# Two attentions and two gate pairs: copies moved behind exponentials, one sum moved ahead of others

## What is computed

```
h = layer_norm(x)
proj = h @ w_in                       # pool, conv, q, kv, k_rope and the logits of three gates
gates = sigmoid(g_logits + b_gate)    # three gates, 1024 wide each: 24 tiles of 128, 12 pairs
y_pool = pool_mixer(u_pool) @ pool_proj        # sliding means minus input, mixed by group
y_conv = conv_module(u_conv) @ conv_proj       # 31 taps, layer norm, silu
y_mla = attention(8 heads, chunk-causal, 64 wide values) @ mla_proj
merged = gates[0] * y_pool + gates[1] * y_conv + gates[2] * y_mla
h = layer_norm(a * h + merged @ w_out)
...                                   # mixture of experts, then a state-space mixer and a conv FFN
h = fox_attention(h)                  # 16 heads, causal, with forget gates
...                                   # output projection, norm, conv FFN, norm
```

## Time and profile before

| | |
|---|---|
| median of 3 runs | 2550.92 us (2550.4 to 2553.96) |
| profiled execution | 2549.24 us |
| its span | 2547.4 us |
| TensorE products busy | 2515.7 us, 99% |
| VectorE busy | 1374.1 us, 54% |
| ScalarE busy | 618.7 us, 24% |
| GpSimd busy | 83.7 us, 3% |
| granted TensorE clock | 0.998 of full |
| first attention | about 173 to 226 us of the span |
| gate pairs | about 219 to 455 us |
| second attention | about 1953 to 2064 us |

### The profile page before, as it was taken

How to read it: one execution, slowest core, us unless ns; L and a number is a source line. 1 busy time by engine, 2 the same in 40 slices (tenths; PEclk the granted TensorE clock), 3 DMA queues, 4 the chain that set the end, 5 groups by cost and what they waited for, 6 DMA issues and landing times.

```text
span 2547.4 us, 31452 instructions
## 1 busy us (share of the span) xinstructions
PE 2515.7 (99%) x10720; PEld 1903.6 (75%) x10720; DVE 1374.1 (54%) x2528; ACT 618.7 (24%) x1406; POOL 83.7 (3%) x117
## 2 busy tenths in 40 slices
PE   9999999999999999999999999999999999999998
PEld 7857878684444467888746888888885668888887
DVE  6778754441111146646385777752361857777633
ACT  3244223120000013222222222210231633222112
POOL 0010000000000010000020000000000200000000
PEclk9999999999999999999999999999999999999999
DMA  4224212248999952222112222224322022222233
GB/s 143 83 81 184 91 61 97 91 182 305 363 336 336 327 187 71 84 90 91 59 50 99 83 83 90 82 91 132 108 89 78 9 67 91 90 83 91 84 117 130
DMA packets 90562, 319.06 MB, mean 125 GB/s; under 512 B 9632, under 2 KB 13856, under 8 KB 90432
## 3 DMA queue, kind: packets, MB, share of 16 engines
q1 hardware_dynamic: 81584, 284.37, 32.4%
q10 hardware_dynamic: 5152, 19.92, 2.0%
q0 software_dynamic: 3728, 13.44, 1.6%
HBM read 295.61 MB, written 22.02 MB: 125 GB/s over the span
## 4 chain that ended last, share of the span: by engine, by line
PE 91%; DVE 5%; ACT 2%; issue 1%; DMA 1%; POOL 0%; ACTq 0%; SPq 0%; DVEq 0%; POOLq 0%
PE bank L924 44%; PE bank L650 13%; PE bank L1198 13%; PE bank L896 4%; PE bank L1069 2%; PE bank L776 2%; PE bank L798 1%; PE bank L1477 1%; PE bank L1347 1%; PE bank L1465 1%; PE bank L825 1%; ACT R L1601 1%; DVE R L3106 1%; PE bank L684 1%; PE bank L1210 1%
## 5 line engine op out<-in xcount | busy, mean ns | idle before, releaser
L924 PE MATMUL bank<-SQ,arena 128*128 128x256 f32 x2040 | 469.8, 379 | 0.0
L924 PEld LDWEIGHTS bank<-SQ,arena 128*128 128x128 f32 x2040 | 387.5, 190 | 52.8 <-DVE arena L2167 0.2
L1198 PE MATMUL bank<-arena 128*128 128x512 f32 x768 | 332.7, 592 | 0.8 <-ACT arena L1844 0.8
L924 PE MATMUL bank<-X,ring 128*128 128x256 f32 x1360 | 322.5, 379 | 0.0
L650 PE MATMUL bank<-arena,ring 128*128 128x256 f32 (+1 forms) x1280 | 319.5, 411 | 0.0
L650 PEld LDWEIGHTS bank<-arena,ring 128*128 128x128 f32 x1280 | 243.2, 190 | 74.9 <-issue 46.6
L924 PEld LDWEIGHTS bank<-X,ring 128*128 128x128 f32 x1360 | 258.2, 190 | 38.4 <-issue 3.6
L1198 PEld LDWEIGHTS bank<-arena 128*128 128x128 f32 x768 | 144.6, 190 | 176.5 <-issue 176.5
L924 PE MATMUL bank<-X,arena 128*128 128x256 f32 x680 | 160.9, 379 | 2.0 <-DVE bank L2189 2.0
L924 PE MATMUL bank<-SQ,ring 128*128 128x256 f32 x680 | 161.1, 380 | 1.2 <-DVE R L2194 0.9
L2189 DVE TENSOR_TENSOR bank<-bank,arena 128x256 f32<-128x256 f32 x97 | 41.9, 432 | 223.1 <-ACT bank L1681 222.8
(11 more groups left out here) (394 smaller groups left out, 3038.8 us busy)
## 6 DMA issues: line engine op xcount, KB each, us to landing
ring<-w_stream SPq DMA_DIRECT2D x326, 512.0 KB, 3.3
arena<-w_stream SPq DMA_DIRECT2D x204, 512.0 KB, 5.1
y_slots<-X ACTq DMA_DIRECT2D x1, 9216.0 KB, 25.8
y_slots<-arena ACTq DMA_DIRECT2D x16, 512.0 KB, 5.1
x_tok<-arena ACTq DMA_DIRECT2D x1, 2048.0 KB, 6.6
out_t<-X SPq DMA_DIRECT2D x16, 128.0 KB, 2.2
X<-x_t SPq DMA_DIRECT2D x1, 1024.0 KB, 8.2
part<-params SPq DMA_DIRECT2D x1, 824.0 KB, 8.9
```

The source lines that it names most:

```text
L924: mm = pe.matmul(out, w(n), v(k), start=start and n == 0, stop=n == len(chunk_pairs(p)) - 1, skip_group_check=not start)
L1198: mm = pe.matmul(ebank(t)[:, :], w_, ERING[:, at:at + S], start=(k == 0), stop=(k == len(lhs) - 1))
```

## The change

Four places are touched.

1. "att": on ScalarE `early()` keeps the latent's value copies, and the pooled chunks with the fill's transfer become `pooled_chunks`, called as `later()` behind both parts of the second head's exponentials.
2. "fatt": on TensorE the last of the six value steps moves from the first extra part to the second one, between the scores of heads 1 and 2. On ScalarE the value copies move from `early()` to `later()`.
3. Both: GpSimd copies the queries of head 2 ahead of its wait for the values.
4. Gate pairs 0 and 8: VectorE makes the third sum ahead of the branch inputs' and next weights' sums. In pair 0 the next pair's weight sums and the branch's sums of weights go behind the fourth output; in pair 8 the weight sums stay ahead of it and the branch's go behind it. The order in the other pairs stays.

```diff
-            attention("fatt", lambda: more_values(2, C8), None,
+            attention("fatt", lambda: more_values(2, C8 - 1), lambda: more_values(C8 - 1, C8),
...
-            def attention(name, early):
+            def attention(name, early, later=None):
...
-                early()
+                if early:
+                    early()
                 exps(1, 0)
                 exps(1, 1)
+                if later:
+                    later()
                 step_of_pair()
...
+
+            def pooled_chunks():
                 for g in range(4):
                     t = A0["poolw"] + g
                     a_ready(act, t)
...
-            attention("att", latent_values)
+            attention("att", latent_values, pooled_chunks)
...
-            attention("fatt", more_values)
+            attention("fatt", None, more_values)
...
                 if p == 0:
+                    third_sum("gates", p)
 
                     for n in range(4):
                         a_read(dve, A0["att"] + 4 * HEADS1 - 4 + n)
                     sums_of_branch_inputs(0)
-                if p < 11:
+                elif p == 8:
+                    third_sum("gates", p)
                     sums_of_weights("gates", p + 1)
-                third_sum("gates", p)
-                if branch:
+                else:
+                    if p < 11:
+                        sums_of_weights("gates", p + 1)
+                    third_sum("gates", p)
                     branch_third_sum(p - 1)
                     branch_first_output(p - 1)
-                if p not in BPLAIN:
+                    if p not in BPLAIN:
+                        sums_of_branch(p)
+                fourth_output("gates", p, GS[:, 2 * (p % 2) + 1, H:S])
+                if p == 0:
+                    sums_of_weights("gates", 1)
+                if not branch:
                     sums_of_branch(p)
-                fourth_output("gates", p, GS[:, 2 * (p % 2) + 1, H:S])
...
                 queries(0)
                 queries(1)
+                queries(2)
                 values_there()
                 columns(0)
                 columns(1)
-                queries(2)
```

## The result

The changed kernel took 2542.12 us (median of 7 executions, 2541.18 to 2553.05), the kernel before 2550.92 (7 executions, 2550.22 to 2555.84).

A forecast was written before the change was run, and what follows sets the result against it. TensorE was taken to bound the kernel, so stalls removed from its stream move all that follows. The terms 1.84+1.44+1.36+0.92 = 5.56 us took 2549.24 to 2543.68, plus 1.68 to the median: 2545.4 us, range 2543.6 to 2548.6.

The forecast's parts named there:

- First attention, 1.84 us: Third head's scores no longer wait for ScalarE's exponentials, so the transposes start at 189.80 instead of 191.64: 1.84 us.
- the scores' 2.16 us: Third head's scores in the attentions take 2.16 us with free banks, instead of 2.39 chasing the exponentials.
- room for the chunks: First attention: ScalarE finishes the moved pooled chunks 0.29 us before its first transposed copy is due.
- The third queries: GpSimd's earlier copy of the third head's queries gains nothing by itself; VectorE's sums beside it may lose 0.3 us.
- the "some 0.3 us" of the sum by that rule: First attention: by the skill's exclusion rule, GpSimd's copy beside VectorE's pooling sums costs the forecast gain some 0.3 us.
- Second attention, 1.44 us: A value step between second and third scores removes TensorE's wait; transposes start at 1986.46 instead of 1987.90: 1.44 us.
- Gate pair 0, 1.36: With VectorE's third sum earlier, four products take 6.92 us instead of 8.28, and nothing new is late: 1.36 us.
- Gate pair 8, 0.92: The same 1.36 us saved, less 0.44 because the next pair's first product waits for ScalarE's second output: 0.92 us.
- no part was lost: Rival, chance 0.20: thin room in the first attention, pair 8 or the scores costs one part; 2546.2 to 2547.2 us.
- nothing was given back: Rival, chance 0.11: the attentions' waits pass to other edges and give nothing; 2.3 us remain, 2548.6 us.
- VectorE caught up: Slower rival, chance 0.07: VectorE's postponed work in pair 0 never catches up, delaying later pairs' weights; 2556 us.
- The sum: Four places, two attentions and two gate pairs, add to 5.56 us; forecast 2545.4 us, 0.22% less.

The follow-up runs named there:

- e8: Changed kernel with ScalarE's four pooled chunks put back ahead of the second head's exponentials in the first attention: 2545.79 us, ratio 0.9982.
- e5: Changed kernel with GpSimd's copy of the third queries put back behind the wait for the values and the column copies: 2546.21 us, ratio 0.9983.
- e9: Kernel before with needless TensorE products filling the stalls in both attentions: 2550.59 us, ratio 0.9997.
- e4: Changed kernel with only the gate pairs' new VectorE order kept, attentions as before: 2550.27 us, ratio 0.9995.
- e7: Changed kernel with TensorE's value products in the second attention put back into one piece: 2547.31 us, ratio 0.9989.
- e3: Changed kernel with only the attentions' edits kept, VectorE's gate order as before: 2545.23 us, ratio 0.9978.
- e2: Kernel before, no edit, profiled a second time: that execution took 2553.66 us.
- e14: Kernel before, no edit, one of three more profiles of one execution each: 2560.7 us.
- e17: Changed kernel again, no edit, timed beside two versions with the routing's products spread: 2543.98 us, ratio 0.9977.
- e11: Changed kernel with the second attention's TensorE and ScalarE edits undone and that stall filled with needless products: 2550.12 us, ratio 0.9987.
- e10: Changed kernel with both halves of the second attention's edit undone, third queries still early: 2547.47 us, ratio 0.9975.

## Why the prediction was wrong

**First attention, 1.84 us: right** (1.86 in the trace). So were its steps: the start of the exponentials within 0.1 us, the scores' 2.16 us, and room for the chunks, 0.93 us instead of 0.29, since ScalarE stops for no mix. e8 undid it alone: 2.1 us at full clock.

**The third queries: right by itself, wrong as costed at nothing.** I looked at the old order, where the queries didn't decide, and not at the new one, where they would have (e5, 2.71 us). The GpSimd copy did slow VectorE's sums beside it, by about what I allowed. The same four sums, first in the kernel before without such a copy, then in the changed kernel:

```profile
174.03 2.92 DVE L2569 TENSOR_TENSOR arena<-arena 128x527 f32<-128x527 f32 x4
```

```profile
174.12 3.20 DVE L2575 TENSOR_TENSOR arena<-arena 128x527 f32<-128x527 f32 x4
...
175.39 0.65 POOL L3279 COPY arena<-arena 96x512 f32<-96x512 f32 x1 [3.26 <-PE bank L798]
```

VectorE loses 0.28 us. It delayed the first maxima by as much (178.78 to 179.16 us, of which 0.1 was there before these sums), ahead of which TensorE had other work, and cost the end nothing. With the rule of the Trainium skill (SBUF — State Buffer, "Who interferes with whom"), the trace agrees in direction; the "some 0.3 us" of the sum by that rule did not come.

**Second attention, 1.44 us: right** (1.46). **Gate pair 0, 1.36: right** (1.37). **Gate pair 8, 0.92: too low** (1.16). From the fifth product's start to the eighth's (the next pair's first) it took 5.30 us in place of 3 x 1.73 = 5.19, so the wait is 0.1, not 0.33. I had carried ScalarE's second output over from the earlier trace rows at its old distance. In the kernel before, the late sixth product and ScalarE's first output were

```profile
389.45 1.99 PE L924 MATMUL bank<-X,arena 128*128 128x256 f32 x8 [0.99 <-DVE bank L2189]
...
390.97 0.47 ACT L1692 ACTIVATE arena<-bank,part 128x256 f32<-128x256 f32 x1
```

and the second came 0.51 us behind it (391.48), when that product had just ended (389.45 + 1.99 = 391.44); in the changed kernel it came 0.37 us behind. No rival of the parts came: no part was lost, nothing was given back, and VectorE caught up.

**The sum is the step that failed**, and in two places. The terms were 0.3 us low, which is small. First, it priced each stall at its own length and what follows a stall at nothing, without a reason. In 5 of 17 cases a stall was followed by TensorE at 1.2 GHz, 1.4 to 3.15 us more, a mean of 1.1 us for the kernel before (an estimate from four falls in 16 places); the one profile that I had showed none. The executions can neither confirm nor refute this mean: with both stalls filled (e9) the kernel before lost 5.0 us to the clock against 5.4, and a mean over 12 executions is uncertain by more than 1 us. Second, "it lay 1.68 us under the median of the runs, so I forecast 2545.4" carried the distance over as if it were an offset. By the profiles, what sets executions apart is mostly clock lost in the routing, which differs between executions by up to 10 us, and which I had not weighed: the windows behind the earlier trace rows are those of the gate pairs. A median of seven then moves by itself: the changed kernel's three sets gave 2542.12, 2544.04 and 2543.98. All 31 together make 2543.59, 7.9 us under the 2551.53 of the kernel before, so 1.5 us of the miss of 3.3 are the low first draw, which is luck. The 2550.92 that I started from was itself 0.6 us low. Of the 2.4 us that are left with this (7.9 measured, 5.56 forecast), the terms are 0.3, the falls behind the stalls some 1.1 in the mean, and 1.0 is not accounted for. Whether the changed kernel loses less clock than the one before beyond these falls isn't settled: the mean granted clock differs by 0.5 thousandths (1.2 us, as much as the falls make), with an interval of -0.1 to 1.2 thousandths. The range reached 1.8 us below the forecast; with this scatter of the medians it should have reached 3 to 4.

**Open:** what decides in which execution the clock falls, in the routing above all. No edit was shown to act on the routing's falls, and e4, e7 and e3, whose routing is the same, lost a mean of 6.7, 7.1 and 2.8 us to the clock.

## What to carry to other kernels

Price a stall of TensorE twice: by its length, and by what the products behind it take if the clock falls in or behind it; a profile of one execution may not show this, so look at two or three. Where executions differ in their granted clock, compare times at equal clock: here that turned 8.8, 8.0 or 6.8 us, depending on the set, into 6.2 plus or minus 0.4, and it showed the gate pairs' 2.7 us (e4), where the interval of the ratio reached 1. And when work is moved behind other work, go through every queue that waits for its results in the new order: a copy that was never late (the third queries) became 2.7 us late.

## What the hardware showed

A stall of 1.2 us was followed by a granted clock of 0.50 for some 6.8 us (e2, e7), yet in 7 of 9 traces the same stall had no such sequel. Behind the first attention's stall (e2, e14) and e5's the clock stayed down for some 3.4 us, and fell only 1.4 to 1.9 us after TensorE had started again. The Trainium skill (TensorE: Matmul & The Clock Gate, "HAM oscillation — how this bites in real kernels") tells of such falls behind waits for DMA, at every step of a loop; here the traces show them behind waits for other engines, in 5 of 17 cases. The clock also fell with TensorE busy in every microsecond of the profile, where products of 16 columns were many: 0.83 and 0.67 over 513 to 553 us in the changed kernel's slowest execution, 10.0 us of its time (134.03 us for the stretch that takes e17 124.02), and not at all in others of the same kernel (e17: 1.00 in the same stretch). That these narrow products are the cause is not shown. Needless products in a stall did not lengthen the stretch around it (1025.51 us in e11, 1025.50 in e10), though e11's executions as a whole were 1.6 us slower at full clock.
